# Delta rule: the inverse of the 16-row key blocks made inside the compression's token loop, stored to DRAM and read back

## What is computed

```python
def compress_kv(kv, pe, w1, w2):
    ...
    blk = blk + pe[None, None, :, None]
    flat = blk.transpose(0, 1, 3, 4, 2, 5).reshape(B, nc, NSA_KV_HEADS, 2, NSA_BLOCK * HEAD_DIM)
    hid = jax.nn.silu(jnp.einsum('bngcf,cfe->bngce', flat, w1))
    return jnp.einsum('bngce,ced->bngcd', hid, w2)

def chunk_gated_delta(q, k, v, g, beta, s0):
    ...
    decay = jnp.exp(jnp.where(tril, G[..., :, None] - G[..., None, :], -jnp.inf))
    kb = k * beta[..., None]
    A = jnp.where(tril & (eye == 0), jnp.einsum('bhncd,bhnsd->bhncs', kb, k) * decay, 0.0)
    Tm = lax.linalg.triangular_solve(eye + A, jnp.broadcast_to(eye, A.shape), left_side=True, lower=True)
    u = Tm @ (v * beta[..., None])
    w = Tm @ (kb * jnp.exp(G)[..., None])
    ...
```

## Time and profile before

| | us |
|---|---|
| median of 3 runs (2939.7 to 2945.09) | 2939.72 |
| the profiled execution's own time | 2935.54 |
| its span, first to last instruction | 2933.8 |
| PE busy in the span | 2793.3 (95%) |
| DVE busy in the span | 2273.9 (78%) |
| ACT busy in the span | 1392.5 (47%) |
| POOL busy in the span | 345.4 (12%) |

### The profile page before, as it was taken

One profiled execution on the slowest core, in us unless ns is written; L12 is line 12 of the kernel. 1 busy time (PEld: TensorE's weight loads), 2 busy tenths in 40 slices (PEclk: granted clock), 3 DMA queues, 4 the chain that ended last, 5 costly groups with the idle time before them and its releaser, 6 DMA issues.

```text
span 2933.8 us, 55557 instructions
## 1 busy us (share of the span) xinstructions
PE 2793.3 (95%) x22669; PEld 2671.0 (91%) x22669; DVE 2273.9 (78%) x3548; ACT 1392.5 (47%) x2385; POOL 345.4 (12%) x322
## 2 busy tenths in 40 slices
PE   8999999989988969999889999999999999999998
PEld 8999999988877658799889999999999999999997
DVE  6766777877677777755688888888888888888898
ACT  5444555555555635532254444444444453434345
POOL 0020000014270214124320000000000000000002
PEclk9999999999999979999999999999999999999998
DMA  7456544458633964463344353534343465434342
GB/s 221 136 149 197 158 111 110 120 190 278 239 117 128 367 168 125 141 185 87 98 157 135 111 142 102 142 111 142 103 142 112 142 190 169 148 113 154 116 147 98
DMA packets 521999, 440.20 MB, mean 150 GB/s; under 512 B 36270, under 2 KB 476773, under 8 KB 515665
## 3 DMA queue, kind: packets, MB, share of 16 engines
q1 hardware_dynamic: 457906, 303.50, 35.9%
q0 software_dynamic: 19568, 80.16, 7.4%
q10 hardware_dynamic: 44272, 52.98, 5.4%
HBM read 378.33 MB, written 66.55 MB: 152 GB/s over the span
## 4 chain that ended last, share of the span: by engine, by line
PE 49%; DVE 5%; issue 1%; ACT 1%; POOL 0%; DMA 0%; ACTq 0%; POOLq 0%; DVEq 0%; SPq 0%
PE i L3386 42%; PE i L140 7%; DVE f_half L3943 1%; DVE x_blocks L3981 1%; DVE h_rows L3976 0%; DVE w_ring L3932 0%; DMA s_h<-resid 0%; DVE x_blocks L3909 0%; DVE f_sum L3936 0%; ACT resid L3569 0%; DVE f_sum L3925 0%; ACT f_half L3636 0%; DVE ln_parts L3987 0%; PE i L3396 0%; ACT x_blocks L3583 0%
## 5 line engine op out<-in xcount | busy, mean ns | idle before, releaser
L3386 PE MATMUL i<-x_blocks,f_half 128*128 128x272 f32 x10752 | 1358.8, 288 | 27.3 <-DVE h_rows L3976 10.7
L3386 PEld LDWEIGHTS i<-x_blocks,f_half 128*128 128x128 f32 x10752 | 1348.7, 189 | 32.9 <-DVE x_blocks L3981 14.6
L570 PE MATMUL a<-xb_in,w_half 128*128 128x272 f32 x4200 | 542.4, 290 | 3.9 <-DVE conv_in L1000 2.0
L570 PEld LDWEIGHTS a<-xb_in,w_half 128*128 128x128 f32 x4200 | 532.0, 188 | 12.7 <-issue 7.2
L3636 ACT CAST f_half<-w_ring 128x1024 fp32r<-128x1024 f32 (+2 forms) x370 | 346.3, 937 | 403.3 <-PE i L3386 340.0
L3943 DVE TENSOR_TENSOR f_half<-w_ring,f_half 128x1024 fp32r<-128x1024 f32 (+2 forms) x362 | 392.7, 1085 | 80.8 <-ACT f_half L3636 78.3
L3943 DVE TENSOR_TENSOR f_half<-f_sum,f_half 128x1024 fp32r<-128x1024 f32 (+2 forms) x148 | 159.4, 1077 | 81.1 <-ACT f_half L3636 81.1
L972 DVE TENSOR_TENSOR w_half<-w_ring,w_half 128x1024 fp32r<-128x1024 f32 x129 | 157.5, 1222 | 75.7 <-ACT w_half L708 75.3
L3636 ACT CAST f_half<-f_sum 128x1024 fp32r<-128x1024 f32 (+2 forms) x148 | 138.7, 937 | 153.1 <-PE i L3386 151.8
L708 ACT CAST w_half<-w_ring 128x1024 fp32r<-128x1024 f32 x125 | 131.3, 1050 | 108.9 <-PE a L570 105.4
L3349 POOL TENSOR_TENSOR f_half<-w_ring,f_half 128x512 fp32r<-128x512 f32 x8 | 12.7, 1583 | 1401.1 <-ACT f_half L3636 1401.1
(11 more groups left out here) (599 smaller groups left out, 4165.3 us busy)
## 6 DMA issues: line engine op xcount, KB each, us to landing
w_ring<-in_ffn_w_up_dram SPq DMA_DIRECT2D x88, 1024.0 KB, 6.8
w_ring<-in_w_in_dram SPq DMA_DIRECT2D x52, 1024.0 KB, 8.8
w_ring<-in_ffn_w_down_dram SPq DMA_DIRECT2D x24, 1536.0 KB, 7.2
w_ring<-in_w_o_dram SPq DMA_DIRECT2D x16, 1024.0 KB, 6.4
x_blocks<-s_blk ACTq DMA_DIRECT2D x17, 816.0 KB, 5.0
s_proj<-st ACTq DMA_DIRECT2D x48, 272.0 KB, 2.8
s_blk<-x_sums ACTq DMA_DIRECT2D x22, 544.0 KB, 6.7
kv_ring<-in_cmp_w_dram SPq DMA_DIRECT2D x16, 512.0 KB, 7.8
```

What stands on the lines that cost most here:

```text
L570: last = nc.tensor.matmul(ps[bank][:, 0:HT2], half(q, w)[:, k], XB[v[j]][:, k], start=j in (0, 1, 3) and k == 0 and i == 0, stop=k == HK - ...
L3386: last = nc.tensor.matmul(ps[bank][:, 0:HT2], half(e, j, wl_)[:, s], XB[:, x0 + s, xl_, BLK_OF[j]], start=start and s == 0 and i == 0, sto ...
```

## The change

The key blocks and the whole row substitution move from the delta rule's prelude into the compression's loop. Their tiles lie in the MIX tile, which is free at that time. The results go to a new DRAM tensor S_inv and come back as the first loads of the delta rule.

- SP, compression: after part 1 of W1 it waits until the projection's rows are stored, then issues two DMAs for KALL (1 MB each), twelve for TAB and one for HB (the mask), all counted on `kb_in`, and only then XP and part 2 of W1. At the end it waits for the two transposes, stores TIC and TTC (512 KB each), and waits for the stores to land before it loads keys and values of the attention over their place.
- PE: half of `key_blocks` after the products of token 6, the other half after those of token 7. The first waits for all fifteen loads. The prompt's rows are turned after tokens 9 and 11 and not 5 and 7.
- DVE: `blocks_log` after `row_lo` of token 4; it waits for all fifteen loads too. `blocks_weights` after token 7, `blocks_keys` after token 8, then at most one product or one sum a token from token 10 to 43 (tokens with a `w_lo` left out; the first four rows take product and sum in one token), and the two transposes after token 44. The prompt's rows are evicted at tokens 9 to 12.
- ACT: one exponential of 128x512 before `row_hi` of token 6.
- POOL: clears XI before its first gather of the block.
- Delta rule: SP loads TIC first and TTC fifth. POOL's `spread` waits for these loads alone for head 0.

The diff, cut to its core:

```diff
 (compression, SP)
+                        rows_stored(sp)
+                        for h in range(0, GH, 4):
+                            first = R_QKV + (GH + h) * P
+                            sp.dma_start(KALL[:, h:h + 4], S_proj[first:first + 4 * P]...).then_inc(kb_in, 16)
+                        for k, rows_ in enumerate((S_rows[0], S_rn[1, GH:2 * GH], S_rn[0, GH:2 * GH])):
+                            for b in range(4):
+                                ...
+                                sp.dma_start(TAB[32 * b:32 * b + 32, k], part).then_inc(kb_in, 16)
+                        sp.dma_start(HB, C_dram[:, AT["hide_b"][0]:AT["hide_b"][1]]).then_inc(kb_in, 16)
                         sp.dma_start(XP, O[2][0, 0].rearrange("(q t) g c d -> t q (g c d)", t=PAGE)).then_inc(xp_in, 16)
...
+                sp.wait_ge(inv_r, 2)
+                sp.dma_start(S_inv[0], TIC.rearrange("p x c -> p (x c)")).then_inc(inv_out, 16)
+                sp.dma_start(S_inv[1], TTC.rearrange("p x c -> p (x c)")).then_inc(inv_out, 16)
...
+                sp.wait_ge(inv_out, 32)
 (compression, PE)
+                def key_blocks(h0, h1):
+                    pe.wait_ge(kb_in, 16 * 15)
...
-                    if t in (5, 7):
-                        prompt(t - 5)
-                        prompt(t - 4)
+                    if t in (6, 7):
+                        key_blocks((t - 6) * GH // 2, (t - 5) * GH // 2)
+                    if t in (9, 11):
+                        prompt(t - 9)
+                        prompt(t - 8)
 (compression, DVE)
+                def blocks_log():
+                    dve.wait_ge(xz, 1)
+                    dve.wait_ge(kb_in, 16 * 15)
...
+                    if t == 4:
+                        blocks_log()
+                    if t == 7:
+                        blocks_weights()
+                    if t == 8:
+                        blocks_keys()
+                    if t in PROD_AT:
+                        block_product(PROD_AT[t])
+                    if t in ROW_AT:
+                        block_row(ROW_AT[t])
+                    if t == BACK_AT:
+                        blocks_back()
+                    if t in (9, 10, 11, 12):
+                        prompt(t - 9)
 (samples' attention, SP: the loads of KALL and TAB are gone)
 (delta rule, SP)
+                sp.dma_start(TIC[:].rearrange("p x c -> p (x c)"), S_inv[0]).then_inc(inv_in, 16)
                 rows_in(0)
                 norm_in(0)
                 qg_row_in(0)
+                sp.dma_start(TTC[:].rearrange("p x c -> p (x c)"), S_inv[1]).then_inc(inv_in, 16)
...
-                    if h == GH // 2:
-                        sp.wait_ge(kx_ps, 1)
 (delta rule, POOL)
-                            gp.wait_ge(x_l, X_DONE + 1)
+                            gp.wait_ge(inv_in, 32)
 (delta rule, PE)
-                        key_blocks(0, GH).then_inc(kx_ps, 1)
 (delta rule, DVE: blocks_log() to blocks_back() are gone)
```

More of the change, by code:

```diff
@@ L1216, in _ @@
             def _(gp):
+                nc.gpsimd.memset(XI, 0.0).then_inc(xz, 1)
                 for u in range(AHEAD, BLK):
@@ L1223, in _ @@
             def _(pe):
+                def key_blocks(h0, h1):
+                    pe.wait_ge(kb_in, 16 * 15)
+                    for h in range(h0, h1):
+                        for t in range(QT):
+                            for b in range(4):
+                                k = KALL[:, h, t * P + 32 * b:t * P + 32 * b + 32]
+                                last = nc.tensor.matmul(KKX[32 * b:32 * b + 32, h * QT + t], k, k, start=True, stop=True)
+                    last.then_inc(kx_ps, 1)
                 def prompt(q):
@@ new lines, in blocks_weights, with blocks_keys @@
+                def blocks_weights():
+                    dve.wait_ge(x_exp, 1)
+                    blocks.link(nc.vector.tensor_tensor(XE, XE, of_rows(1), ALU.mult))
+                    blocks.link(nc.vector.tensor_tensor(XE, XE, of_cols(2), ALU.mult))
+                def blocks_keys():
+                    dve.wait_ge(kx_ps, 2)
+                    last = nc.vector.transpose(XK.rearrange("p (c s) -> p c s", s=32), KKX.rearrange("p x c -> p c x"))
+                    last.then_inc(kx_r, 1)
+                    dve.wait_ge(kx_r, 1)
+                    for k in range(NB_X):
+                        a = k * BASE_B
+                        x = XK.rearrange("p (c s) -> p c s", s=32)[:, a:a + BASE_B, a:a + BASE_B]
+                        last = nc.vector.scalar_tensor_tensor(XE[:, k], x, -1.0, XE[:, k], ALU.mult, ALU.mult)
+                    blocks.link(last)
@@ L1334, in w_lo, with blocks_back @@
+                def blocks_back():
+                    turned_ = XI[:, 0:1024].rearrange("p (s c) -> p s c", s=32)
+                    nc.vector.transpose(TIC.rearrange("p x s -> p s x"), turned_).then_inc(inv_r, 1)
+                    nc.vector.transpose(TTC.rearrange("p x c -> p c x"), turned_.rearrange("p s c -> p c s")).then_inc(inv_r, 1)
                 def w_lo(i):
@@ L2206, in build @@
             GLP = sb(ph, "gl_p", [P, QT, GH])
[L2207 to L2210, removed]
+            ps = banks(ph, "g")
             D_BANKS = (3, 0)
@@ L2361, in _ @@
                 nc.tensor.matmul(ps[0][:, 0:B * GH], ones[0:NS, :], GM[:].rearrange("p b h -> p (b h)"), start=True, stop=True).then_inc(gl_ps, 1)
-                def key_blocks(h0, h1):
-                    for h in range(h0, h1):
-                        for t in range(QT):
-                            for b in range(4):
-                                k = KALL[:, h, t * P + 32 * b:t * P + 32 * b + 32]
-                                last = nc.tensor.matmul(KKX[32 * b:32 * b + 32, h * QT + t], k, k, start=True, stop=True)
-                    return last
                 def products_y(h, l):
@@ L2926, in s_mixed @@
                                                    ALU.mult, ALU.mult).then_inc(fin_s, 1)
-                blocks_log()
                 s_decay()
@@ L2945, in _ @@
                 s_placed()
-                for c in range(10, BASE_B):
-                    block_row(c)
-                blocks_back()
                 for i in range(GH + 2):
```

126 lines of the change are left out of this document (56 added, 70 removed).

## The result

The changed kernel takes 2953.42 us (median of 6 runs, 2948.89 to 2958.45) against 2940.84 us of the kernel before (6 runs, 2936.77 to 2945.09). The ratio is 1.0046, with an interval of 1.0035 to 1.0057: slower by 0.46%, 12.6 us between the medians. Forecast were 2948.7 us and plus 9.0.

A forecast was written before the change was run, and what follows sets the result against it. PE was taken to bound the compression's loop and DVE the delta rule's prelude. 19.6 us paid in the compression less 10.6 gained in the delta rule gave +9.0, so 2948.7 us, range 2935 to 2956.

The forecast's parts named there:

- Landing of the fifteen loads: Compression, tokens 4 to 5: DVE, then PE, wait for loads landing at about 666; 11.6 us paid, between 4.6 and 16.6.
- rival A: Compression: the loads land in time, so wait and clock loss go; -4.1 us, 2935.6; chance 0.22.
- Tokens 5 to 13: Compression loop after the wait: key blocks 4.0, clock 1.5 and delay by blocks_keys 0.5; 6.0 us paid.
- Key blocks: Compression, PE: their busy time now falls in a loop without idle PE; 4.0 us paid, upper end 7.8.
- the cold clock: Compression, PE after the stop: the granted clock falls to the 1.2 GHz level; 1.5 us paid, lower end 0.
- Products and sums: Compression, DVE: fifteen products and sums fit its free time between tokens; costed at nothing.
- Two transposes: Compression, DVE after token 44: 3.8 us at once, partly covered by PE's lead; 2.0 us paid, between 0 and 3.8.
- Delta rule: Prelude and the gap before it: 9.6 + 2.9 - 1.9 for TIC = 10.6 us gained, between 3.6 and 11.7.
- The gap at the end of the samples' attention: Between DVE's last attention work and the delta rule: earlier last loads save 2.9 of 4.9 us, between 0 and 3.4.
- the unexplained wait of the earlier trace: Delta rule's prelude, PE: 2.24 us no semaphore explains, taken to go with the key blocks, within the 9.6 gained.
- Rival B: Delta rule: head 0 still starts late, by sample-state loads or the unexplained wait; gain 3.6, +16.0 us, 2955.7; chance 0.12.
- Rival C: Compression: PE waits for instructions in both halves of the key blocks; 7.6 us more, 2956.3; chance 0.08.

The follow-up runs named there:

- e9_hold: Against the changed kernel, POOL issues gather 8 and those behind it only after the fifteenth load has landed; 2947.7 us, ratio 1.0026.
- e3_tic: Against the changed kernel, SP loads TIC fifth, behind rows and norms of head 0 and ahead of TTC; 2950.56 us in one execution.
- e1_late: Against the changed kernel, the fifteen loads go behind XP and part 2 of W1, and everything using them comes later; 2933.54 us, 0.9984 of the kernel before.
- e2_split: Against the changed kernel, the two transposes become four halves after tokens 44, 46, 47 and 48; 2949.19 us in one execution.
- e7_all: Against the changed kernel: late consumers, key blocks in eight pieces, transposes in four halves, sample states loaded ahead of head 1; 2929.15 us, 0.9962 of the kernel before.
- e4_queue: Against the changed kernel, ACT issues the twelve TAB loads and HB on its own queue, KALL stays on SP; 2949.94 us, ratio 1.0034.
- e6_states: Against the changed kernel, SP loads the sample states ahead of head 1's rows and norms in the delta rule; 2949.21 us, ratio 1.0035.

## Why the prediction was right, and where its sizes were off

Direction, places and mechanism held. The median lies within the stated 2935 to 2956, and 0.4 us above the 2944 to 2953 of the forecast itself. The net was forecast at +9.0 and measured at +12.6: the compression paid 26.3 us where the sum had 19.6, the delta rule gave 11.9 where it had 10.6, and 1.4 came from the step between them, which the sum did not have.

- **Landing of the fifteen loads: 11.6 forecast, 13.8 measured.** KALL was well sized: 23.7 us after the block's start by the packets of the earlier trace rows, about 23 by the counts. The step that failed is "while PE stands, POOL gets no free tile to gather into, so its queue runs empty; I take a third, 2.4". POOL had issued ten gathers between 642.9 and 658.3, more than PE had taken; they kept q0 busy until 667, so TAB and HB took 3.1 us behind KALL in place of 2.4, and in e9_hold, where q0 had run empty, 0.9. A second step is short too: DVE went on 1.9 us after the last packet, at 28.1 in place of 26, where XP, whose landing the sum started from, needed 0.7 (last packet at 655.5, landed at 656.3). From the landing to PE's products the forecast was 3.4 us, measured 3.47.
- **The 6.15 us per MB** of the Trainium skill, "DMA: Bandwidth & Descriptors", section Bandwidth, give an estimate of 12.3 us for KALL, by which rival A would have been right. The trace does not agree: KALL, issued at 643.80, was through some 21 us later, 5 of them behind part 1 of W1 in its own queue and some 16 beside the gathers. The same page's section "Queues, rings and completion order" says that an engine takes the queues in turn, a packet at a time; the DMA rows agree, in what the profile counts as packets: 283 against 279, with 1.03 MB against 0.57. Taken together with the queue of gathers already issued, that rule fits the late landing.
- **Tokens 5 to 13: 6.0 forecast, 8.4 measured.** Key blocks 3.9 (1.50 + 0.85 + 0.91 of wait + 0.67), as taken. The other 4.5, where I had 2.0, are the cold clock and four stops of 0.41 to 1.54 us for `row_lo`, after `blocks_keys` and after the prompts' evictions, which I called "only moved": beside `blocks_keys` DVE no longer has its lead. An estimate from the steps of tokens 5 and 6 (4.26 us, and 4.60 with 1.43 of key blocks, against 2.26 for a token at full clock) puts 2.9 of the 4.5 down to the clock, where I had 1.5, and leaves 1.6 to the stops, where I had 0.5.
- **Products and sums: 0 forecast, 0.00 measured** over 31 tokens.
- **Two transposes: 2.0 forecast, 4.1 in this trace, 2.6 in four others at the same place, 0 in halves.** The cover was judged nearly rightly; that so short a stop may also cost clock was not considered.
- **Delta rule: 10.6 gained by forecast, 11.9 measured** (10.33 to the first product, 1.67 given back behind it, 3.2 at the block's end). The gap at the end of the samples' attention fell from 4.95 to 1.75 us of DVE's idle time, 3.2 saved where 2.9 were forecast. TIC delayed the scaled keys by 2.2 us (1.9 forecast), but that price is not on the path, as e3_tic shows. From the scaled keys on 12.5 us went, not 9.6: the unexplained wait of the earlier trace rows is gone as taken, and the clock is better, 1.00 in 1098 to 1106 against 0.63 in 1072 to 1085 before, so that the last of the work ahead of head 0 takes 1.94 in place of 3.59 us. It is not this execution alone: the eight other kernels reach head 0's first product 22.6 to 25.8 us after the block's first work, against 24.84 here and 35.17 before. The sum had no such term, and none for the 1.67 us given back; that the two partly cancel is luck.
- **Rival A** falls: the loads landed 11 us behind its point (668.2 in the frame of before, against 657). **Rival B**'s mechanism is there, the states became the bound of the prelude, but it takes 1.5 us of the gain and not 7. **Rival C**'s wait came in the change with 0.91 us in one half only, in e1_late, where the granted clock was 1.00 in the 14 us up to it, with 2.67, and in e9_hold in both halves, with 0.51 and 1.96.

## What to carry to other kernels

A wait put into a loop costs what stands behind it on the same list, so the question is when the last byte lands; count what is already issued on the other queues, since an engine that stops does not take its issued transfers back. Work moved into gaps of another engine is free as long as each piece fits one gap plus the lead of its consumer: 30 small operations cost nothing here, two of 2 us cost 2.1 to 4.8, and the same two in four pieces 0 (e2_split) and 0.25 (e7_all). When a gain is measured at one mark, check that PE waits at that mark.

## What was not expected of the hardware

- A queue whose issuer has stopped still held 65% of the engines' time and more for some 8 us (q0, 658.3 to 666).
- A run of quick 32-column products stops after 90 to 203 records, for 0.4 to 3.8 us, with no semaphore to explain it, and not at all in pieces of 32.
- A stop of 2.3 us on PE was followed by products of 0.63 us, the 1.2 GHz level, in the change; in e3_tic, e4_queue, e6_states and e9_hold, behind the same stop, the step from token 45 on took its normal 2.26 us.
